# Attention by pairs of heads, one-step token shift, decay from running sums and two modulation slots per pair in a fused two-block transformer

## The reference, cut to what matters

```python
def first_block(x, ...):                # one pooling layer, then one attention layer, each with a SwiGLU FFN
    x = x + pool_mixer(rmsnorm(x, ...), pool_w, pool_scale)
    x = x + swiglu(rmsnorm(x, ...), w_gate_up[0], w_down[0])
    k, v = split(rmsnorm(x, kv_norm) @ w_kv);  q = rmsnorm(x, ...) @ w_q[0]
    # 16 heads of 64: softmax(q k^T / 8 + bias(distance), causal) v      <- attention 1
    x = x + o @ w_o[0]
    x = x + swiglu(rmsnorm(x, ...), w_gate_up[1], w_down[1])
    return rmsnorm(x, final_norm)

def hybrid_layer(x, c, ...):            # the second block
    mod = silu(c) @ ada_w + ada_b       # 6144 numbers: shifts, scales and gates
    z = (rms_norm(x) * (1 + sc1) + sh1) @ w_in
    q, k, v, iq, ik, iw, zr, ga, gr = split(z)
    attn = dsa_sparse_attention(...)    # an indexer takes the 64 best keys of each query, then
                                        # 8 heads of 64 over them                          <- attention 2
    zr = zr + mu * (shifted_by_one_token(zr) - zr)          # token shift
    decay = exp(-exp(-softplus(-(w0 + tanh(wd) @ up)) - 0.5))
          # = exp(-exp(-0.5) * sigmoid(w0 + tanh(wd) @ up))
    # a delta rule over the tokens in chunks of 64 needs, in each chunk, the product of the
    # decays up to each token, that up to the token before, and the inverse of the first
    mixed = sigmoid(ga) * (attn @ w_attn_br) + sigmoid(gr) * (rw @ w_rwkv_br)
    x = x + g1 * (mixed @ w_out)
    x = x + g2 * moe_ffn(...)           # 64 experts, 8 of them a token, and a shared one
```

## Time and profile before

| | us |
|---|---|
| median of 3 runs | 1512.92 (1512.19 to 1520.71) |
| the profiled execution | 1521.38, its span 1519.7 |
| PE busy | 1407.3 (93%) |
| DVE busy | 718.3 (47%) |
| ACT busy | 505.3 (33%) |
| POOL busy | 171.8 (11%) |
| chain that ended last: PE, DVE, ACT | 83%, 13%, 2% |

### The profile page before, as it was taken

One profiled execution on the slowest core, in us unless ns is written; L12 is line 12 of the kernel. 1 busy time (PEld: TensorE's weight loads), 2 busy tenths in 40 slices (PEclk: granted clock), 3 DMA queues, 4 the chain that ended last, 5 costly groups with the idle time before them and its releaser, 6 DMA issues.

```text
span 1519.7 us, 24624 instructions
## 1 busy us (share of the span) xinstructions
PE 1407.3 (93%) x10441; PEld 1065.8 (70%) x10444; DVE 718.3 (47%) x1180; ACT 505.3 (33%) x820; POOL 171.8 (11%) x76
## 2 busy tenths in 40 slices
PE   5998997999999999799698887999999999999995
PEld 3998997974799999699697776974444444444432
DVE  5764766444156666668976445451211212122113
ACT  2532434533434334256353223332222222222213
POOL 0000000000000000176772004600000000000000
PEclk7999999999999999999898898899999999999998
DMA  9755353239944554303325023325999999999993
GB/s 362 312 191 185 132 200 126 56 159 425 412 166 167 189 185 166 125 1 84 125 85 232 20 86 141 117 85 234 422 427 425 424 423 425 427 425 424 424 428 123
DMA packets 37508, 363.42 MB, mean 239 GB/s; under 512 B 5027, under 2 KB 6179, under 8 KB 8740
## 3 DMA queue, kind: packets, MB, share of 16 engines
q1 hardware_dynamic: 36692, 359.55, 59.0%
q0 software_dynamic: 720, 2.46, 0.8%
HBM read 359.30 MB, written 2.69 MB: 238 GB/s over the span
## 4 chain that ended last, share of the span: by engine, by line
PE 83%; DVE 13%; ACT 2%; issue 2%; DMA 0%; POOL 0%; DVEq 0%; SPq 0%; ACTq 0%
PE banks L1054 14%; PE banks L592 12%; PE banks L593 12%; PE banks L594 12%; PE banks L1079 8%; PE banks L1014 4%; PE banks L1005 4%; DVE scr L1676 2%; PE banks L674 2%; PE banks L718 2%; PE banks L570 2%; DVE ring L1665 1%; PE banks L857 1%; PE banks L648 1%; PE banks L631 1%
## 5 line engine op out<-in xcount | busy, mean ns | idle before, releaser
L592 PE MATMUL banks<-h_hi,gu_hi 128*128 128x256 f32 x704 | 201.1, 286 | 5.1 <-issue 5.1
L593 PE MATMUL banks<-h_lo,gu_hi 128*128 128x256 f32 x704 | 200.3, 284 | 0.0
L594 PE MATMUL banks<-h_hi,slot_lo 128*128 128x256 f32 x704 | 200.1, 284 | 0.0
L592 PEld LDWEIGHTS banks<-h_hi,gu_hi 128*128 128x128 f32 x704 | 136.3, 194 | 5.7 <-issue 5.6
L593 PEld LDWEIGHTS banks<-h_lo,gu_hi 128*128 128x128 f32 x704 | 136.4, 194 | 0.1
L594 PEld LDWEIGHTS banks<-h_hi,slot_lo 128*128 128x128 f32 x704 | 136.2, 194 | 0.0
L1930 DVE TENSOR_TENSOR out_lo<-banks,out_hi 128x512 fp32r<-128x512 f32 x64 | 44.3, 692 | 190.1 <-ACT out_hi L1406 190.1
L594 PE MATMUL banks<-slot_lo,slot_lo 128*128 128x256 f32 x416 | 118.8, 286 | 0.0
L1079 PE MATMUL banks<-ring,scr 128*64 128x512 f32 x512 | 116.9, 598 | 1.9 <-ACT scr L1400 1.9
L1054 PE MATMUL banks<-ring,scr 128*64 128x512 f32 x512 | 112.6, 592 | 0.0
L1054 PE MATMUL banks<-ring 128*64 128x512 f32 x512 | 112.6, 592 | 0.0
(11 more groups left out here) (403 smaller groups left out, 3161.0 us busy)
## 6 DMA issues: line engine op xcount, KB each, us to landing
ring<-ws SPq DMA_DIRECT2D x93, 1536.0 KB, 7.5
ring<-experts SPq DMA_DIRECT2D x64, 2048.0 KB, 11.1
ring<-experts SPq DMA_DIRECT2D x64, 1024.0 KB, 10.8
ring<-experts SPq DMA_DIRECT2D x1, 3072.0 KB, 11.2
scr<-bias_line POOLq DMA_DIRECT2D x4, 512.0 KB, 8.0
bias_line<-scr SPq DMA_DIRECT2D x1, 1536.0 KB
x<-xT SPq DMA_DIRECT2D x1, 1024.0 KB, 4.8
scr<-pool_w SPq DMA_DIRECT2D x1, 1024.0 KB, 7.5
```

Source lines behind the costliest of these rows:

```text
L592: nc.tensor.matmul(out, hi, move_hi, start=start, stop=False, skip_group_check=True)
L593: nc.tensor.matmul(out, hi, move_lo, start=False, stop=False, skip_group_check=True)
L594: return nc.tensor.matmul(out, lo, move_hi, start=False, stop=stop, skip_group_check=True)
```

## The change

Four things change together.

1. Both attentions go by pairs of heads. A step of the loop is a pair: PE issues the two first score products on the two row halves one behind the other into B[0] and B[1], then the two second ones, six transposes into B[2] and B[3], and the products with the values on the two column halves. PE now transposes in step j the pair j-1 (before: head j-2), and multiplies with the values of pair j-1 (before: head j-3). DVE takes scores, mask and maxima of both heads with one instruction over two banks each; the four multiplications with the reciprocals stay single. ACT keeps single exponentials and copies both heads' transposed probabilities at once. There are two buffers of two heads for the scores and one for the transposed probabilities.
2. In attention 1 a step takes two modulation slots. Three products of zeros clear B[5] to B[7] ahead of it, so that one activation can copy 97 rows, and 12 products of 97 rows by four columns of the identity replace the 48; they stand in one piece ahead of the norm's sum.
3. ACT copies each tile of zr out twice, once times 1 - mu into its place and once times mu; DVE adds the neighbours with one instruction for 12 tiles.
4. DVE adds up the decay rates by a scan, and ACT forms from the sums the three exponentials (product, product before, inverse) at tile EXP_AT = 32. The copy, the shift and the reciprocal on DVE go.

```diff
@@ TensorE: attention
-                for j in range(heads + 3):
...
+                for j in range(heads // 2 + 1):
+                    if j < heads // 2:
+                        if n0 + j:
+                            pe.wait_ge(s_used, n0 + j)
+                        for p in range(2):
+                            nc.tensor.matmul(B[p][:, 0:T], qT[rows(p), j, P:T], kT[rows(p), j, :], start=True, stop=True)
+                        for p in range(2):
+                            mm = nc.tensor.matmul(B[p][:, T:T + P], qT[rows(p), j, 0:P], kT[rows(p), j, 0:P], start=True, stop=True)
+                        mm.then_inc(s_ready, 1)
+                    if j >= 1:
+                        a = j - 1
                         pe.wait_ge(p_ready, n0 + a + 1)
...
+                        for p in range(2):
+                            for d, s in ((0, T), (P, 0), (2 * P, P)):
+                                mm = nc.tensor.transpose(B[2 + p][:, d:d + P], ex[:, a % 2, p, s:s + P], ident)
                         mm.then_inc(pt_ready, 1)
-                    if between is not None and j < heads:
+                    if between is not None and j < heads // 2:
                         between(j)
-                    if j >= 3:
-                        a = j - 3
+                    if j >= 1:
+                        b = o_banks[a % len(o_banks)]
                         pe.wait_ge(pts_ready, n0 + a + 1)
...
@@ TensorE: modulation
+            def two_modulations(j):
+                modulation(2 * j)
+                modulation(2 * j + 1)
...
+            for b in range(5, 8):
+                nc.tensor.matmul(B[b], zeros[:, 0:P], zeros[:], start=True, stop=False, skip_group_check=True)
+            attention(HEADS_1, 0, q1, k1, v1, ex, pts, B[4:5], between=two_modulations)
...
-            pe.wait_ge(mod_copied, 4)
-            for q in range(4):
-                if q == 2:
-                    norm_sum(3)
-                for j in range(3):
-                    for t in range(4):
-                        row = slice(32 * q, 32 * q + 1)
-                        mm = nc.tensor.matmul(mod_products(q)[:, 4 * j + t:4 * j + t + 1], modrow[row, j, t * P:(t + 1) * P], ones[row, 0:1], start=True, stop=True)
+            pe.wait_ge(mod_copied, 1)
+            for j in range(3):
+                for t in range(4):
+                    mm = nc.tensor.matmul(mod_products[:, j, :, t], modrow[mod_rows, j, t * P:(t + 1) * P], ident[mod_rows, 0:P:32], start=True, stop=True)
             mm.then_inc(mod_turned, 1)
+            norm_sum(3)
@@ ScalarE
-                    act.wait_ge(act_step, AC)
-                    nc.scalar.activation(b1, b1, ACT.Exp, scale=-math.exp(-0.5)).then_inc(decay_ready, 1)
...
+                if i == EXP_AT:
+                    act.wait_ge(decay_ready, DECAY_SUMS)
+                    nc.scalar.activation(power, b1, ACT.Exp, scale=-math.exp(-0.5))
+                    nc.scalar.activation(power_before[:, :, 1:], b1[:, :, 0:T - 1], ACT.Exp, scale=-math.exp(-0.5)).then_inc(act_step, 1)
+                    act.wait_ge(act_step, 1)
+                    nc.scalar.activation(b1, b1, ACT.Exp, scale=math.exp(-0.5)).then_inc(decay_ready, 1)
...
+                    nc.scalar.activation(zs[:, c, :], PROJ_BANKS[u % 3][:, 0:T], ACT.Copy, scale=keep[:, c:c + 1])
+                    nc.scalar.activation(d, PROJ_BANKS[u % 3][:, 0:T], ACT.Copy, scale=vcol("tshift_mu", c)).then_inc(proj_used, 1)
@@ VectorE: attention
+                for j in range(heads // 2 + 1):
+                    if j < heads // 2:
+                        e, two_heads = ex[:, j % 2], slice(2 * j, 2 * j + 2)
                         dve.wait_ge(s_ready, n0 + j + 1)
...
+                        nc.vector.scalar_tensor_tensor(e[:, :, late], banks[:, 0:2, late], HEAD ** -0.5, bias[:, two_heads, :], ALU.mult, ALU.add)
+                        m = nc.vector.scalar_tensor_tensor(e[:, :, early], banks[:, 0:2, early], HEAD ** -0.5, bias[:, two_heads, P:T], ALU.mult, ALU.add)
...
+                        nc.vector.tensor_reduce(nmax[:, j % 2, 0, :], e[:, :, late], AX_X, ALU.max, negate=True)
+                        nc.vector.tensor_reduce(nmax[:, j % 2, 1, :], e[:, :, early], AX_X, ALU.max, negate=True).then_inc(max_ready, 1)
                     if j >= 1:
+                        a = (j - 1) % 2
+                        dve.wait_ge(exp_ready, n0 + j)
+                        then(nc.vector.reciprocal(rrec[:, a], rsum[:, a]))
+                        for p in range(2):
+                            for b, cols in ((0, late), (1, early)):
+                                ins = nc.vector.tensor_scalar(ex[:, a, p, cols], ex[:, a, p, cols], rrec[:, a, b, p:p + 1], None, ALU.mult)
+                        ins.then_inc(p_ready, 1)
@@ VectorE: token shift and decay
-            shift_differences(0, 12)
-            shift_mixed(0, 6)
-            shift_mixed(6, 12)
+            token_shift(0, 12)
...
+            dve.wait_ge(decay_ready, DECAY_RATES)
+            per_chunk(lambda c: nc.vector.tensor_tensor_scan(b1[:, c, :], chunk_mask, b1[:, c, :], 0.0, ALU.mult, ALU.add))
+            dve.sem_inc(decay_ready, 1)
...
-            per_chunk(lambda c: nc.vector.tensor_tensor_scan(b2[:, c, :], b1[:, c, :], b3[:, c, :], 0.0, ALU.mult, ALU.add))
-            nc.vector.tensor_copy(p_end, starts(b2)[:, :, :, CH - 1])
-            then(nc.vector.tensor_copy(b3[:, :, 1:], b2[:, :, 0:T - 1]))
-            then(nc.vector.memset(starts(b3)[:, :, :, 0:1], 1.0))
-            then(nc.vector.reciprocal(b1, b2))
```

More of the change, by code:

```diff
@@ L218, in build, with by_pair @@
         hq = sq
-        ex, pts = view(2048, 3, 384), view(3200, 2, 384)
-        nmax, rsum, rrec = small[:, 2:8], small[:, 8:14], small[:, 14:20]
+        def by_pair(a):
+            return a.rearrange("p (b h s) -> p b h s", b=2, h=2)
+        ex, pts = by_pair(view(2048, 4 * 384)), view(3584, 2, 384)
+        nmax, rsum, rrec1, rrec2 = (by_pair(small[:, lo:lo + 8]) for lo in (2, 10, 40, 20))
         q1, k1, v1, bias1 = view(4352, KC, T), view(6400, KC, T), view(8448, TB, D), view(10496, HEADS_1, T)
@@ L275, in build @@
         gst, rhs_u, u_sb = view(8480, 2, AC, CH), view(8992, AC, CH), view(9248, AC, CH)
+        keep = small[:, 20:34]
+        power, power_before, chunk_mask = view(6432, AC, T), view(7456, AC, T), rinv[:]
         p_end = small[:, 40:56].rearrange("p (a b) -> p a b", a=AC)
@@ L623, in attention, with rows @@
             def attention(heads, n0, qT, kT, v, ex, pts, o_banks, between=None):
[L625 to L634 removed]
+                def rows(p):
+                    return slice(p * HEAD, (p + 1) * HEAD)
@@ L710, in _ @@
             pe.wait_ge(csil_ready, 1)
-            attention(HEADS_1, 0, q1, k1, v1, ex, pts, B[4:5], between=modulation)
+            for b in range(5, 8):
+                nc.tensor.matmul(B[b], zeros[:, 0:P], zeros[:], start=True, stop=False, skip_group_check=True)
+            attention(HEADS_1, 0, q1, k1, v1, ex, pts, B[4:5], between=two_modulations)
             pe.wait_ge(o_copied, HEADS_1 // 2)
@@ L812, in _ @@
             pe.wait_ge(bonus_used, 1)
-            attention(HEADS_2, HEADS_1, q2, k2, v2, ex2, pts2, B[4:6])
+            attention(HEADS_2, HEADS_1 // 2, q2, k2, v2, ex2, pts2, B[4:6])
             pe.wait_ge(o_copied, (HEADS_1 + HEADS_2) // 2)
@@ L1230, in _ @@
             act.wait_ge(w_used, S_O)
-            for q in range(4):
-                nc.scalar.activation(modrow[32 * q:32 * q + 1, :, :], banks[32 * q:32 * q + 1, 5:8, :], ACT.Copy).then_inc(mod_copied, 1)
+            nc.scalar.activation(modrow[mod_rows, :, :], banks[mod_rows, 5:8, :], ACT.Copy).then_inc(mod_copied, 1)
             ffn_start(S_FFN2)
@@ L1309, in _ @@
             nc.scalar.activation(b6, banks[:, 6:8, :].rearrange("p a (b t) -> p (a b) t", b=2), ACT.Copy)
-            attention(HEADS_2, HEADS_1, o2, ex2, pts2, B[4:6])
+            attention(HEADS_2, HEADS_1 // 2, o2, ex2, pts2, B[4:6])
             def pair_bank(b0):
@@ L1599, in _ @@
             dve.wait_ge(bias_loaded, 16 * P // SHIFTS)
-            attention(HEADS_1, 0, bias1, None, ex)
+            attention(HEADS_1, 0, bias1, None, ex, rrec1)
             def modulation_columns():
```

139 lines of the change are left out of this document (62 added, 77 removed).

## The result

The changed kernel takes **1532.17 us** (median of 4 runs, 1529.24 to 1532.62) against 1513.1 (4 runs, 1512.19 to 1520.71) before: ratio **1.011**, 95% interval 1.008 to 1.015. The forecast was 1516, range 1504 to 1542. It is slower by 1.1%, and the interval reaches from 0.8 to 1.5%. I had put 0.62 on no change beyond 1% and 0.33 on slower than that.

What follows compares the result with a forecast made beforehand. PE's own chain was taken to bound attention 1, with low clock in attention 2 and a PE wait for DVE's token shift. Terms 4.3 + 10 + 7 + 1.5 - 7 - 13 = +3 on median 1512.92 gave 1516 us, range 1504 to 1542.

Steps and rivals of the forecast that it cites:

- no change beyond 1%: Whole kernel: the time stays within 1% (15 us) of before; chance 0.62.
- slower than that: Whole kernel: slower by more than 1%, if the clock stays away or two slots cost 3.62 us; chance 0.33.
- Attention 1, +14.3 forecast: Attention 1: PE waits 3.3 us a pair for DVE, +4.3 us at full clock; six idles cost the clock, +10.
- The rival that the clock stays away (1540): Attention 1: clock not back within a pair's 5.3 busy us, pairs 13.5 us instead of 8.6, whole 1540; chance 0.30.
- The rival that it stays up: Attention 1: the idles do not cost the clock, so the +10 falls away, whole 1506 us; chance 0.15.
- Attention 2, +7 forecast: Attention 2: a wait of 4.3 us a pair, at the low clock, makes it 38.3 us against 31.1.
- Behind it +1.5 forecast: Behind attention 2: the delta rule's first products start at 1.2 GHz, +1.5 us, bounds 0 and 3.
- Modulation, -7 forecast: Before the second FFN: 24 records turned instead of 96, root and reciprocal now open; -5.3 to -7.2 us, taken as -7.
- Token shift and decay, -13 forecast: Second half's projections: the 10.9 us idle before the head sums and the low clock behind it go; bounds -14 and -10.
- the squares of the keys are ready by 742 at the latest even if POOL slows DVE threefold: Projections: without the 19.57 us of mixing, DVE has the keys' squares before PE comes at 744.9.
- the prediction's own sign of being wrong: Wrong if DVE multiplied pair j-1 before pair j's scores came, or a stretch outside the four moved over 3 us.
- the likeliest case: Whole kernel: the forecast itself, chance 0.50, alone 1510 to 1525 us.

Runs made afterwards that it cites:

- fill_before_low_rank: The changed kernel with 8 products of zeros ahead of the wait for the last relu before the low-rank products; 1524.58 us, ratio 1.007.
- fill_idle: The changed kernel with 12 products of zeros between a pair's scores and the wait for p_ready, in attention 1 alone; 1517.56 us, ratio 0.998.
- norm_first: The changed kernel with DVE multiplying pair j-1's exponentials before it takes pair j's scores, in both attentions; 1504.7 us, ratio 0.993.
- fill_attention_2: The changed kernel with multiplication first in attention 1, attention 2 by heads, and 6, 10 and 4 zero products behind its first three heads' scores; 1492.4 us, ratio 0.986.
- all_together: fill_both with DVE's four multiplications by k_k, and those by k_a, each made one operation; 1493.14 us, ratio 0.983.
- fill_both: fill_attention_2 with the 8 products of zeros before the low-rank wait as well; 1492.99 us, ratio 0.984.
- one_op_per_vector: The changed kernel with multiplication first in attention 1, attention 2 by heads, and DVE's four multiplications by k_k, and by k_a, as one; 1496.92 us, ratio 0.987.

## Why the prediction was right, and where it was not

**Attention 1, +14.3 forecast, +15.0.** The mechanism and both sizes held: 78.3 us, forecast 68.1 + 10; the forecast had taken the attention before as 63.8 instead of 63.3. Idles of 3.3 us (forecast 3.3), seven of them, and behind each 3.4 us at 1.2 GHz (forecast 3.4, in six). The Trainium skill (TensorE: Matmul & The Clock Gate, Why this matters for your kernels) would have all seven cost, which was +12 instead of +10; all seven did here, six of seven in fill_before_low_rank. The rows of before had three idles to hold against it, not two: those of 2.74 and 3.1 us cost the clock, that of 1.8 did not. Two slots at full clock are 2.69, against 2.6 from the loads of the earlier trace rows. fill_idle leaves the wait and takes the low clock away: the forecast's split, 4.3 at the full clock and 10 for the clock, measures 4 and 11. norm_first takes the wait away and with it 20.6 us. The rival that the clock stays away (1540) falls: it came back within every pair. The rival that it stays up falls too.

**Attention 2, +7 forecast, +6.0**, at the low clock as taken; 10.1 us a pair, forecast 10.6. **Behind it +1.5 forecast, +4.2**: the delta rule's first stretch is 6.83 us against 5.82, 1.0 of it. The rest is in small pieces and not settled; the traces show that the low clock some 77 us behind the delta rule's start lasted 10.2 us after (927.9 to 938.2) and 3.4 before (924.4 to 927.9).

**Modulation, -7 forecast, -5.7**: near the lower of its bounds (-5.3 to -7.2). The norm's sum kept its 5.26, with the clock at 0.62 on the mean from 430 to 434. In norm_first, fill_idle and fill_attention_2 the clock stayed at 1.00 there, though nothing of this piece is edited in them, and the piece is 37.0 us instead of 38.7, -7.4; the second FFN behind it is 1.6 us shorter as well. Chain of waits of norm_first:

```profile
407.58 3.57 PE banks L576 x16
```

So the forecast's best case was there to be had, and the execution's clock decided on it. The other eight kernels with the new modulation, the changed one among them, have 38.7.

**Token shift and decay, -13 forecast, bounds -14 and -10; -5.6.** This is the step that failed, in two places. First, "the squares of the keys are ready by 742 at the latest even if POOL slows DVE threefold": the group of four multiplications took 9.62 us instead of 1.14, eight times, since the price is by the instruction and these are short. I took a factor from one row (1.63 us for 256 columns against 0.42, which is nearly four and not three) and applied it to other operations, when what POOL costs is a sum for each instruction. And the 1.63 is a mean over two kinds. The row's twelve instructions are seven of 2.5 to 2.6 us, up to the end of GpSimd's work at 751.05, and five of 0.47 behind it. The line's summary in the trace of before already had both (durations in ns, shortest, median and longest):

```profile
L1665 DVE SCALAR_TENSOR_TENSOR ring<-ring,vecs,scr x14: 471/1480/2628, 694.9 to 752.8; 128x256 f32<-128x256 f32 x14
```

The squares came at 745.05 (741.73 + 3.32), three later than my latest. Second, I took an idle of 1.8 us that had cost nothing as free; in the changed kernel the same idle was 2.04 and left PE 10 us at half clock, 5 us of work. The two hide each other: with the low stretch PE comes late and doesn't wait for DVE; fill_before_low_rank removed the one and met the other.

**The baseline.** The sum, +3, was put on the median (1516), rightly, as the stall of 5 us was in the profiled execution only and lay in none of my four stretches. By the letter of the prediction's own sign of being wrong, that a stretch outside the four moves by more than 3 us, the piece ahead of attention 1 did (-6.9), and this stall is why. Of the 16 us between forecast and measurement the table has 11.8: 7.4 in the projections, 2.7 behind attention 2, 1.3 in the modulation, 0.7 in attention 1, 0.7 in the second FFN, and -1.0 in attention 2. Of the rest, 3 are that the profiled execution of after (1529.24) is below that kernel's other three (1532.12 to 1532.62), and 1.4 that the one of before, without its 6.9, would be 1514.5 and not 1513.1. Where these executions differ, the traces here can't show.

So the terms of the attentions were right, and the sum was 16 us too low because the gains that were to pay for the pairs came out smaller. The case of no change beyond 1%, called likeliest, was missed narrowly (1.1%), and the likeliest case's own range, 1510 to 1525, by 7 us. That the time lay in the whole range, 1504 to 1542, is in part luck: its upper end stood for a rival, the clock that stays away, which did not come true.

## What to carry to other kernels

When one engine's step holds both what the next engine needs at once (here the multiplications of the last pair) and what nobody waits for yet (the scores of the next), put the first ahead: 20.6 us in attention 1 here, and nothing in attention 2, where what followed lay open too. Grouping two heads lengthens the step (from an estimated 1.96 to 3.3 us) and so the wait. Price an idle of TensorE by the work behind it at half speed, and where the wait can't be moved, fill it with products of zeros: 20 of them were worth 5.7 us in attention 2, 84 of them 11 in attention 1. Before crediting the end of a wait, lay the timelines of all engines over the new time: work that ran alone while everybody waited will then run beside GpSimd. And look at single durations before taking a mean from a row.

The fastest by ratio are all_together and fill_both (pairs in attention 1 with the multiplication first, heads in attention 2, fillings), 0.983 and 0.984 of the time before; their intervals overlap with those of the three kernels at 0.986 (fill_attention_2 among them, which has the lowest median, 1492.4 us).

## What the runs showed of the hardware

- Four operations of DVE on 128x256 took 1.14 us with GpSimd idle and 9.62 beside its subtractions, one on 128x1024 1.23 and 3.3, and four scans 2.44, 4.60, 8.85 and 10.99 as they fell less or more beside it.
- Meanwhile GpSimd's subtractions (128x1024) took 2.5 us each with DVE's instructions at 256 columns (after) and 3.4 with those at 1024 (one_op_per_vector): GpSimd is slowed in turn.
- An idle of 3.3 us in front of mixed work cost the clock in seven cases of seven in the changed kernel and in six of seven in fill_before_low_rank. One of 1.86 at the start of attention 1 did in six of the seven kernels with norm_first's order there (not in fill_attention_2), where one of 1.78 in the projections before had not the earlier trace rows, and one of 2.03 or 2.04 in four kernels of eight. In that range the price of an idle was not to be read from its length.
- All kernels have the DMA share at 1.00 in attention 1. At 57.7 us (norm_first, 419 GB/s) PE waits twice for a transfer, 1.9 us in all, at 63.3 (before) not once. That the transfers are the next limit there is argued from this; no run tested it.
